# At the end of each mixture-of-experts layer, the down product of expert 30 moves ahead of the gate and up products of expert 31

## The reference

```python
def hier_moe(x, w_group, b_group, w_expert, b_expert, w_gate, w_up, w_down):
    ...   # each token picks one of 4 groups, then 2 of the group's 8 experts: 32 experts in all
    def run_block(args):
        xb, e = args                                    # rows of tokens, one expert's number
        hid = jax.nn.silu(xb @ w_gate[e]) * (xb @ w_up[e])   # 1024 -> 512, twice
        return hid @ w_down[e]                               # 512 -> 1024
    ...   # the rows are weighted and added back to their tokens
```

## Time and profile before

| | |
|---|---|
| median of three runs | 1788.2 us (1785.87 to 1789.37) |
| profiled execution: its own time | 1785.87 us |
| profiled execution: span | 1784.2 us |
| PE busy | 1683.3 us (94%) |
| DVE busy | 652.7 us (37%) |
| ACT busy | 381.2 us (21%) |
| moved by DMA | 513.81 MB |
| mean granted TensorE clock | 0.97 of full speed |

### The profile page before, as it was taken

One profiled execution on the slowest core, in us unless ns is written; L12 is line 12 of the kernel. 1 busy time (PEld: TensorE's weight loads), 2 busy tenths in 40 slices (PEclk: granted clock), 3 DMA queues, 4 the chain that ended last, 5 costly groups with the idle time before them and its releaser, 6 DMA issues.

```text
span 1784.2 us, 27891 instructions
## 1 busy us (share of the span) xinstructions
PE 1683.3 (94%) x9786; PEld 827.0 (46%) x9787; DVE 652.7 (37%) x1597; ACT 381.2 (21%) x878; POOL 219.3 (12%) x313
## 2 busy tenths in 40 slices
PE   7899889989899999999998899999899999999995
PEld 5466655545444444444433445455444444444332
DVE  2334487832422222222221656764322222222214
ACT  2233355521111111111110234342011111111112
POOL 1232025400000100000010201000001010101000
PEclk9899999999899999999999899999899999999997
DMA  6153049884479999999997800135599999999994
GB/s 187 53 157 110 28 139 305 268 318 180 157 319 414 421 413 421 410 420 412 422 411 323 321 1 1 34 130 227 222 414 419 417 419 418 418 415 415 409 388 163
DMA packets 84883, 513.81 MB, mean 288 GB/s; under 512 B 20821, under 2 KB 43302, under 8 KB 58586
## 3 DMA queue, kind: packets, MB, share of 16 engines
q1 hardware_dynamic: 66378, 463.45, 64.5%
q0 software_dynamic: 18416, 49.16, 8.4%
HBM read 499.65 MB, written 26.52 MB: 295 GB/s over the span
## 4 chain that ended last, share of the span: by engine, by line
PE 76%; DMA 11%; DVE 6%; issue 2%; ACT 2%; DVEq 1%; SPq 1%; ACTq 1%; POOLq 0%
PE ps L2083 68%; DMA mem<-in_moe_w_up 8%; PE ps L2088 8%; DMA mem<-in_cache_mla 2%; ACT mem L801 1%; DVE mem L1366 1%; SPq L482 1%; DVE mem L1861 0%; ACTq L978 0%; DMA mem<-in_mla_w_a 0%; DMA mem<-moe_rows_back 0%; DVE mem L1832 0%; DVEq L1374 0%; DMA mem<-in_mla_wq_b 0%; DVE mem L1824 0%
## 5 line engine op out<-in xcount | busy, mean ns | idle before, releaser
L2083 PE MATMUL ps<-mem 128*64 128x512 f32 (+14 forms) x8402 | 1519.2, 478 | 56.2 <-ACT mem L801 14.3
L2083 PEld LDWEIGHTS ps<-mem 128*64 128x64 f32 (+5 forms) x8402 | 663.8, 146 | 825.5 <-issue 743.6
L801 ACT ACTIVATE mem<-ps 128x512 f32<-128x512 f32 (+7 forms) x358 | 193.5, 546 | 550.8 <-PE ps L2083 378.4
L2088 PE MATMUL ps<-mem 64*128 64x64 f32 (+3 forms) x1384 | 202.5, 281 | 37.1 <-DMA mem<-in_x_prompt 6.8
L2088 PEld LDWEIGHTS ps<-mem 64*128 64x128 f32 (+3 forms) x1384 | 168.2, 182 | 123.1 <-issue 95.5
L1700 DVE TENSOR_TENSOR mem<-mem,ps 64x512 f32<-64x512 f32 x64 | 44.2, 690 | 423.9 <-ACT mem L1044 423.9
L736 POOL DMA_INDIRECT moe_rows_back<-mem x64 | 57.3, 896 | 826.6 <-DVE mem L1718 805.0
L1044 ACT ACTIVATE mem<-ps 64x512 f32<-64x512 f32 x64 | 37.7, 589 | 547.0 <-PE ps L2083 547.0
L1366 DVE STREAM_TRANSPOSE mem<-mem 128x2560 f32<-128x2560 f32 x32 | 89.2, 2824 | 16.6 <-DMA mem<-in_cache_mla 16.4
L1718 DVE COPY mem<-ps 64x512 f32<-64x512 f32 x64 | 44.4, 693 | 135.4 <-PE ps L2083 135.2
L686 POOL DMA_DIRECT2D mem<-in_cache_mla x96 | 51.5, 537 | 75.9 <-PE ps L2083 68.7
(11 more groups left out here) (240 smaller groups left out, 518.3 us busy)
## 6 DMA issues: line engine op xcount, KB each, us to landing
mem<-in_moe_w_gate SPq DMA_DIRECT2D x64, 2048.0 KB
mem<-in_moe_w_up SPq DMA_DIRECT2D x64, 2048.0 KB
mem<-in_moe_w_down SPq DMA_DIRECT2D x64, 2048.0 KB
mem<-in_cache_mla POOLq DMA_DIRECT2D x160, 160.0 KB, 3.6
mem<-in_cache_mla SPq DMA_DIRECT2D x96, 160.0 KB, 4.4
mem<-moe_rows_back SPq DMA_DIRECT2D x8, 1024.0 KB, 8.9
mem<-in_mla_wkv_b SPq DMA_DIRECT2D x8, 512.0 KB, 5.8
mem<-in_mla_wo SPq DMA_DIRECT2D x1, 4096.0 KB, 14.2
```

Of the source, the lines that this page charges most:

```text
L801: return act.activation(out, in_, ACT.Copy)
L2083: return pe.matmul(out, lhsT, rhs, start=start, stop=stop)
L2088: return pe.transpose(out, in_, ident[at:at + n, at:at + n])
```

## The change

The last few steps of the loop over experts stand in another order in three of the engines' programs, and nothing else is changed. PE does `down` of expert 30 before `gate_up` of expert 31. ACT copies the first half of expert 30's result before the silu of expert 31. DVE copies the second half of it before it multiplies and copies the hidden values of expert 31. Both layers run this code.

```diff
@@ ACT, in experts(L)
                 follow(MADE - 2, 1)
+                rows_back_0(NE - 2, NE // 2 - 1, 0)
                 silu(NE - 1, 1)
-                rows_back_0(NE - 2, NE // 2 - 1, 0)
                 rows_back_0(NE - 1, NE // 2 - 1, 1)
@@ DVE, in experts(L)
                 follow(MADE - 2, 1)
+                rows_back_1(NE - 2, NE // 2 - 1, 0)
                 hidden(NE - 1, 1)
                 hidden_T(NE - 1, 1)
-                rows_back_1(NE - 2, NE // 2 - 1, 0)
                 rows_back_1(NE - 1, NE // 2 - 1, 1)
@@ PE, in experts(L)
                     follow(NE // 6 - 1, r)
+                down(NE // 6, 0)
                 gate_up(NE // 6, 1)
-                down(NE // 6, 0)
                 turns(NE // 6, 1)
                 down(NE // 6, 1)
```

## The result

The changed kernel took 1798.6 us (median of five, 1795.1 to 1803.0), the kernel before 1789.4 us beside it; the ratio is 1.0067, 95% interval 1.0045 to 1.0090. By the ratio it is slower by some 12 us, where 8.2 had been forecast. The two medians are only 9.2 us apart; all thirty executions of the changed kernel on record have a median of 1802.5 us, and that fits the ratio better. From here on, a difference in us is the ratio's; the medians of five rounds can differ from it by up to 3 us. Its profiled execution took 1796.66 us, span 1795.0, and is one of the fastest.

What follows compares the result with a forecast made beforehand. PE's chain was taken to bind, nearly with DMA, waiting for expert weights at the loops' ends. Layer 1 +7.4 and layer 0 +0.8 gave +8.2 us, 1796.4 us on the median of 1788.2; range 1791.5 to 1801.

Steps and rivals of the forecast that it cites:

- the step for layer 0: Behind layer 0's loop: last store 6.7 us later, read back only +1.9, clock returns 1.1, leaving +0.8 us.
- The mechanism and layer 1: Layer 1's end: `down(30)` waits for its matrix, +5.1; clock +0.9; silu and multiplication uncovered +1.4; sum +7.4 us.
- Nothing takes it back: Behind layer 1's `down(31)`: store, read back and sums wait in turn, so the full +7.4 us reaches the end.
- Rivals 1 and 2: Down of 30 lands before 1732.6 (total -1.6 us, chance 0.06), or within about 1.5 us behind up of 31 (+3.8, 0.10).
- rival 1: At `down(30)`'s wait: its matrix is there in time and PE's wait is filled; total -1.6 us, 1786.6, chance 0.06.
- The 3.46: Layer 1's time from last store to read back, taken for layer 0's store meeting free DMA engines; 3.46 us.
- the 4.9 us that were to come back: Layer 0, last store to read back: 3.46 us instead of 8.35, since the wqkv transfer's tail is over by then.
- the 1.1 that was booked: Layer 0's `hidden(0)` and first projection: less idling ahead, so 1.1 of 2.7 us lost to the low clock returns.
- rival 3: Layer 0 and the clock give nothing back: 7.4 + 6.7 = 14.1 us, 1803 to 1806 with slow `down(31)`; chance 0.08.
- the give-back behind the store: Layer 0's later store no longer shares DMA engines with the wqkv tail, so +6.7 us becomes +1.9 at the read back.

Runs made afterwards that it cites:

- only layer 0: The new order in layer 0 alone, layer 1 as in the kernel before; ratio 1.0040 against the kernel before, +7.2 us.
- again: The changed kernel timed once more with no edit; 1803.3 us, ratio 1.0072 against the kernel before.
- only layer 1: The new order in layer 1 alone, layer 0 as in the kernel before; 1795.8 us, ratio 1.0033 against the kernel before.
- the run with the matrix there: Changed kernel, but `down(30)` uses expert 29's landed matrix; the wait for expert 30's stands before `down(31)` and SP's second wqkv part; 1787.3 us, ratio 0.9992.
- the same, second: The new order in layer 0 alone, run a second time; 1793.3 us, ratio 1.0020 against the kernel before, +3.6 us.
- the filled kernels: Changed kernel with 8 unused products before `down(30)`, ratio 1.0052 against the kernel before; a second with 1 more before expert 31's transposes, ratio 1.0045.

## Why the prediction was right and wrong

The forecast was 1796.4 us, with 1791.5 to 1801 as its range, +8.2 us. By the ratios it is +12 and +12.9, and the median of thirty executions, 1802.5, lies above the range. Layer 1 came out as reckoned; the step for layer 0 failed.

**The mechanism and layer 1: right.** Down of 30 landed 5.4 to 5.7 us behind up of 31 in seven places (both layers of two traces of the changed kernel, one in each of the three with one layer alone), where 5.1 was forecast from the DMA's rate. The trace of the kernel before has 5.5 in both layers already (957.02 and 1739.42, the last landings of the matrix), so the larger distance could have been read from it. The block took 12.4 and 12.7 in layer 1 (forecast 13.1), the gap of the transposes is 1.65 us (forecast 1.4), and `down(31)` kept 3.65. From the landing of up of 31 to the end of `down(31)`: 1751.17 - 1733.92 = 17.25 before, 1762.90 - 1737.84 = 25.1 after, +7.8 against +7.4. Some 0.25 of that is PE's start, 0.29 us behind the landing instead of 0.04.

"Nothing takes it back" was wrong by a little in this pair of traces. From the last store to the end of the span there are 31.4 us before and 30.5 after, and in the chain the 12 records of the last product account for it: 7.96 us before, 6.82 after. Before:
```profile
1763.57 7.96 PE ps L2083 x12
```
After:
```profile
1775.53 6.82 PE ps L2083 x12
```
7.8 - 0.9 = +6.9 for layer 1. Over all traces, from the landing of up of 31 to the end of the span: 50.3, 49.8 and 50.2 us in the three with the old order in layer 1 (before, twice only layer 0), 57.2, 57.4 and 57.7 in the three with the new (after, again, only layer 1), +7.3 in the mean. Measured with that layer alone: +5.9 (3.9 to 8.1).

**Rivals 1 and 2: excluded.** In the kernel itself the landing is 5.4 us or more behind up of 31, not before it and not within 1.5. In the run with the matrix there, rival 1's condition was made true. It gave -1.4 us (-3.4 to +0.7) where the price was -1.6; that isn't told from 0, and the agreement may be luck, since the price assumed a clock that holds: with the slow `down(31)`, the last store of layer 1 came 0.7 us earlier in its trace, and the first projection of layer 0 ended 1.1 us later.

**Layer 0: the term that failed.** The step was "Layer 0: 1.9 - 1.1 = +0.8 us". From the landing of up of 31, in us:

| | before | forecast | after | again | only layer 0 | the same, second |
|---|---|---|---|---|---|---|
| to the last store | 19.5 | 26.2 | 26.3 | 28.5 | 29.1 | 29.1 |
| `down(31)` | 3.65 | 3.65 | 3.65 | 5.01 | 5.19 | 5.21 |
| last store to read back | 8.35 | 3.5 | 4.80 | 4.65 | 4.17 | 4.83 |
| to the start of `hidden(0)` | 36.0 | 37.9 | 39.7 | 41.7 | 41.8 | 42.5 |
| to the end of the first projection | 47.9 | 48.7 | 51.9 | 53.9 | 54.0 | 54.7 |

The last row gives +4.0, +5.9, +6.1 and +6.8 instead of +0.8 (the old order again, in layer 0 of the trace with only layer 1 changed: 48.1), and the times of layer 0 alone +3.6 and +7.2. Three parts of it were mis-sized:
- `down(31)` behind the new gap of 1.65 us ran partly at half clock in three of these four traces, +1.4 to +1.6. The forecast named it (0, at worst 3.6) and chose 0. The block lost up to 3.1 in layer 0 (13.51 against 10.45) instead of 2.65.
- The store needs 4.2 to 4.8 us to its read back. The 3.46 came from layer 1. Of the 4.9 us that were to come back, 3.5 to 4.2 did: +0.7 to +1.4. The big transfer had ended before the store was issued in all four traces; what still moves, the 19 GB/s from 978 to 980 included, are the store's own packets. `--dma` has beside them, in layer 0 (976.09 to 979.50) and not in layer 1, one packet of the instruction queue; the last number is us from issue to landing:
```profile
q8 instruction: 1, 0.02, 2.8%
moe_rows_back<-mem POOLq DMA_INDIRECT x1, 3.9
```
  Layer 1 of the same trace (1764.51 to 1767.98):
```profile
moe_rows_back<-mem POOLq DMA_INDIRECT x1, 2.5
```
  By the packet records, these 16 KB take from 1.2 us behind the store's issue until 2.1 to 2.7, and the store's last packet ends 0.6 to 0.7 us behind them in each of the four traces (2.8 to 3.4), against 2.2 in layer 1. That points to this packet; but the store is larger in layer 0, too (148 KB against 111), and no run takes either away. Another 0.4 us lies between the read back and `hidden(0)` (8.5 to 8.6 against 8.2; the old order has 8.6 too, in the trace with only layer 1 changed).
- The clock gave nothing back. PE's idling before `hidden(0)` fell from 6.28 to 3.14 us, and the transposes gained (1.66 for 1.95), but the fall of the clock only came later: it was at 0.50 from 983.7 to 993.9 before, from 989.9 to 996.7 after, and from some 993 to 1000 in the other three traces. So it lay on the projection, whose 16 records took 9.25, 8.92, 9.51 and 8.91 us against 8.65. The forecast had them shorter (and its 6.9 us at full clock are 7.13 in the filled kernels). That is the 1.1 that was booked and 0.3 to 0.9 more.

The sum: 7.3 for layer 1 and 4.0 to 6.8 for layer 0 make 11.3 to 14.1 us, beside the measured 12 to 13. So rival 3 (layer 0 gives nothing back) was nearer as to the time, and the forecast as to the mechanism: the give-back behind the store is there, and clock losses on other records eat it. The Trainium skill (page "TensorE: Matmul & The Clock Gate", section "What's actually happening") puts the ramp's penalty for modelling at under 1% of a typical kernel's span. These losses are under 1% of the span too, but not small beside this change: with both gaps filled +8.1 us is left of 12 to 13. A slip in the forecast's chances: by its own words slower has 0.76 + 0.08 + 0.06 = 0.90, and it says 0.88.

**Open:** why `down(31)` falls to half clock in some executions and not in others (where PE waits unfilled for down of 30, the slow ones, 5.01 to 5.21, stand behind blocks of 13.1 to 13.5 us, the others, 3.65, behind blocks of 12.0 to 12.7; why, no run shows), and whether layer 0 costs 4 or 7 us in the mean; two runs of five rounds give 3.6 and 7.2, the traces 4.0 to 6.8.

## What to carry to other kernels

Before an operation is moved ahead to fill a wait, read from the issuing queue whether its own operand stands ahead of or behind the one that is waited for; if behind, the change trades one wait for a longer one, and its price is the distance of the two landings. Count also what the old order covered (here silu and the multiplication), and give the clock a price on both sides of each new gap: a loss that is cured on one group of records can turn up on the next. Where a later stage is to give time back, take its latency from that stage and not from the quiet end of the kernel.

## What was not expected of the hardware

- A low clock can be shifted by filler and not only avoided. With the idle stretch of 7 to 9 us ahead of it filled, the block of 48 ran in 10.52 us at full clock and the next 16 records in 6.55 and 5.35 instead of 3.65; with the next gap of 1.65 us filled too, these 16 took 3.65, and in layer 0 the fall was left to the filler behind the loop (11.40 against 9.71 us).
- With only 0.76 us idle ahead of the block (the run with the matrix there), `down(31)` still took 6.60 and 5.30 us behind the gap of 1.65.
- At the end of a queue of 2 MB transfers the DMA engines are far apart: before the change, with up of 31 landed in layer 1, DMA still moved 147 GB/s for 10 us, 1.47 MB of the 4.2 MB of the two matrices behind it, and yet these landed 5.5 and another 4.9 us later (5.4 to 5.7 us for the first in the changed kernels).
